# Head norm of an attention unit placed in the next unit's softmax, key rounded before the next weight piece, rotation product order exchanged

## The chip, the cores and the metric

The kernel runs on one core of one Trainium2 chip. The metric is the time of one execution in microseconds (us). Three executions of the kernel before took 3260.85, 3261.77 and 3262.95 us, so its median is 3261.77 us.

The engines named below are TensorE (PE, matrix products into PSUM), VectorE (DVE), ScalarE (ACT), GpSimd (POOL) and SyncE (SP, which issues the loads of the weights). SBUF is the working memory, PSUM the memory that TensorE writes. Each engine works through its own list of instructions in order; between engines, semaphores say what is ready.

## The reference

Two transformer blocks are applied one after the other to 512 tokens of width 1024, each with two layers. The change touches only the first block's differential attention (four heads, each with two score maps):

```python
def differential_attention(q, k, v, lam_full, subln_g, lambda_init):
    ...
        s = jnp.einsum('bqhcd,bkhcd->bhcqk', qblk, kk, preferred_element_type=jnp.float32) * scale
        p = jax.nn.softmax(s, axis=-1)
        a = p[:, :, 0] - lam_full * p[:, :, 1]
        return jnp.einsum('bhqk,bkhe->bqhe', a.astype(v.dtype), v)
    o = lax.map(block, qb)
    ...
    o = rms_norm(o, subln_g, SUBLN_EPS) * (1.0 - lambda_init)
    return o.reshape(B, S, H * 2 * Dh)
```

Queries and keys get a rotary embedding first:

```python
def apply_rope(t, cos, sin):
    ...
    t1, t2 = tf[..., :half], tf[..., half:]
    return jnp.concatenate([t1 * c - t2 * s, t2 * c + t1 * s], axis=-1).astype(t.dtype)
```

The dilated attention that follows uses the same embedding. Everything is float32.

## The kernel before, in words

**Layout.** Activations stand transposed: features on the 128 partitions, the 512 tokens along the free dimension. Every large product is computed by `gemm` (L451) as three products of split numbers: each operand is a rounded part ("Hi") and what is left ("Lo"), and TensorE computes Hi*Hi, Lo*Hi and Hi*Lo, so a projection of 128 output features is 8 x 3 = 24 matmuls of 128x512, written to one of the two slots of the PSUM tile `psG`.

**Weight pieces.** A projection reads one weight piece ("chunk") of 128x1024. SP loads pieces into a ring of four (`wring`), ACT rounds a piece (`cut_high`, L418, called by `follow`, L420, which first waits until the projection of an earlier piece is done), POOL subtracts (`cut_rest`, L440, tile `wLo`). Two cut pieces are held at a time. `follow(act, c, ...)` cuts piece c+2. SP reloads a slot of the ring when POOL has cut its piece.

**A unit.** The first block's layer has four units of differential attention, one per head (`attend(i)`, a loop on every engine; both layers run them). A unit's order on TensorE is: scores 0 and 1 (eight matmuls), gate projection, transposes of the value, scores 2, transposes 0 of the softmax, scores 3, query projection of the next head ("Q"), transposes 1 and 2, half of the key projection of the next head ("K"), transposes 3, second half of K, the attention output (`d_OUT`, L856), half of the value projection ("V"), two small sums of squares for the head norm (L864), second half of V. The scores and the transposes are numbered 0 to 3 by their block of 128 queries. Transposes 3 are the boundary that the prediction counts from; their row is the second of the two with L827 that have a wait after the query projection.

**The softmax of a unit.** DVE: `largest(n)` (L1341, largest score, from PSUM). ACT: `expo(n)` (L1055). DVE: `combine(n)` (L1349 to L1354: one over the sums, times lambda, the two maps scaled and added; tile `soft`). Then TensorE transposes (L827) and ACT copies out (`out_T`, L1062). `combine(n)` lets transposes n go.

**Rotary embedding.** ACT copies a projection from PSUM in four pieces of 32 partitions, exchanged (`rope_turn`, L1011, tile `tmp`). DVE's `rope_add` (L1301) multiplies that copy by the sine table (L1303), the projection in PSUM by the cosine table (L1304, tile `ra`), and adds (L1311, tile `qk`). The multiplication that reads PSUM frees its `psG` slot. TensorE's V projection needs the slot that K leaves.

**The next unit's scores** need the split query and key: ACT rounds (`cut_q`, L1026; `cut_k`, L1034, tile `kHi`), DVE subtracts (`rest_q`, L1318; `rest_k`, L1325, tile `kLo`).

**The head norm of a unit.** ACT squares the attention output (L1093) and copies it to `oaT`; TensorE sums over the head's 128 features (L864); ACT takes the root (L1101, two halves); DVE takes the reciprocal of each half (L1379, 128x256) and multiplies `oaT` (L1381). `oaT` of all four heads is read only after the dilated attention.

Nothing but the written order of each engine's code and the semaphores sets the order of the work.

## Time and profile before

| | |
|---|---|
| median of three executions | 3261.77 us |
| the profiled execution's own time | 3261.97 us |
| its span, first to last instruction | 3260.1 us |
| outside of the span | 1.9 us |
| mean granted clock of TensorE | 0.996 of full speed |
| TensorE busy | 3181.9 us, 98% |
| VectorE busy | 1641.8 us, 50% |
| ScalarE busy | 1343.6 us, 41% |
| GpSimd busy | 1373.1 us, 42% |

The busy times are sums over the whole span. They say which engine has the most work in total, not which one a stage waits for: that stands in the rows with an idle time and the name of what ended it. The differential attention takes from about 46 to 190 us in the first layer, and from about 1021 to 1165 us in the second.

### The profile page before, as it was taken

The page shows a single profiled execution, that of the slowest core. Times are in us where ns is not written, and L with a number is a line of the kernel's source. Part 1 is how long each engine was busy: PE and PEld are TensorE (multiplying, and loading weights), DVE is VectorE, ACT ScalarE, POOL GpSimd, SP SyncE. Part 2 cuts the span into 40 slices and gives each one's busy share as a digit, 9 for nine tenths or more (in the row PEclk, how much of TensorE's full clock was granted, in tenths as well). Part 3 has the DMA queues.
Part 4 walks back from the last instruction along what each step waited for, and adds up shares of the span by engine and source line. Part 5 has one row for each costly group of instructions (what it writes and reads, how often), then busy time and mean ns, then how long its engine had stood idle before and what let it go on. Part 6 is the DMA issues. An engine that isn't in the chain of part 4 may idle for free. (4 is left out here: it accounts for less than half of the span.)

```text
span 3260.1 us, 45286 instructions
## 1 busy us (share of the span) xinstructions
PE 3181.9 (98%) x15946; PEld 2534.8 (78%) x15946; DVE 1641.8 (50%) x2597; ACT 1343.6 (41%) x2108; POOL 1373.1 (42%) x694
## 2 busy tenths in 40 slices
PE   9999999999999999999999999999999999999999
PEld 6778887788887778887788886777888867778887
DVE  6853337655627853337656624863333248533332
ACT  6765554322226765554322224453222244532222
POOL 3233334544453223334444454544444535444444
PEclk9999999999999999999999999999999999999999
DMA  3122222255522122222255523202223232122222
GB/s 141 58 81 88 81 87 78 104 184 202 188 102 80 58 81 88 87 82 76 103 197 189 193 97 107 78 27 78 97 97 101 99 112 72 33 84 97 95 98 90
DMA packets 93593, 333.26 MB, mean 102 GB/s; under 512 B 10864, under 2 KB 12080, under 8 KB 93232
## 3 DMA queue, kind: packets, MB, share of 16 engines
q1 hardware_dynamic: 91760, 325.52, 28.9%
q10 hardware_dynamic: 1728, 6.36, 0.5%
q8 instruction: 64, 1.05, 0.1%
q14 instruction: 41, 0.34, 0.0%
HBM read 329.69 MB, written 8.44 MB: 104 GB/s over the span
## 5 line engine op out<-in xcount | busy, mean ns | idle before, releaser
L440 POOL TENSOR_TENSOR wLo<-wring,wHi 128x1024 fp32r<-128x1024 f32 x482 | 1174.2, 2436 | 1709.4 <-ACT wHi L418 1709.1
L464 PE MATMUL psG<-hHi,wHi 128*128 128x512 f32 x2992 | 1184.6, 396 | 12.6 <-DVE ra L1304 4.3
L464 PE MATMUL psG<-hLo,wHi 128*128 128x512 f32 x2992 | 1170.1, 391 | 9.1 <-POOL hLo L489 8.2
L464 PE MATMUL psG<-hHi,wLo 128*128 128x512 f32 x2992 | 1165.9, 390 | 0.0
L418 ACT ACTIVATE wHi<-wring 128x1024 fp32r<-128x1024 f32 x482 | 510.2, 1059 | 964.3 <-PE psG L464 934.6
L464 PEld LDWEIGHTS psG<-hHi,wHi 128*128 128x128 f32 x2992 | 562.3, 188 | 152.9 <-issue 33.2
L464 PEld LDWEIGHTS psG<-hLo,wHi 128*128 128x128 f32 x2992 | 561.7, 188 | 141.2 <-POOL hLo L489 23.4
L464 PEld LDWEIGHTS psG<-hHi,wLo 128*128 128x128 f32 x2992 | 562.7, 188 | 113.1 <-issue 0.5
L464 PE MATMUL psG<-hidLo,wHi 128*128 128x512 f32 x704 | 273.9, 389 | 0.0
L464 PE MATMUL psG<-hidHi,wHi 128*128 128x512 f32 x704 | 273.9, 389 | 0.0
L464 PE MATMUL psG<-hidHi,wLo 128*128 128x512 f32 x704 | 273.9, 389 | 0.0
L2340 DVE TENSOR_TENSOR tmp<-tmp,psG 128x512 f32<-128x512 f32 x44 | 30.3, 688 | 298.5 <-PE psG L464 298.5
L1303 DVE TENSOR_TENSOR tmp<-tmp,ropes 128x512 f32<-128x512 f32 x64 | 44.3, 692 | 253.0 <-ACT tmp L1011 253.0
L1011 ACT ACTIVATE tmp<-psG 32x512 f32<-32x512 f32 x256 | 151.1, 590 | 30.8 <-PE psG L464 27.4
L464 PEld LDWEIGHTS psG<-hidHi,wHi 128*128 128x128 f32 x704 | 132.1, 188 | 28.0
L464 PEld LDWEIGHTS psG<-hidHi,wLo 128*128 128x128 f32 x704 | 132.1, 188 | 27.3
L464 PEld LDWEIGHTS psG<-hidLo,wHi 128*128 128x128 f32 x704 | 132.1, 188 | 27.2
L1409 DVE CUSTOM_DVE_ANT_0 soft<-psS,mask 128x768 f32<-128x768 f32 x64 | 61.0, 953 | 154.6 <-issue 154.6
L1484 DVE CUSTOM_DVE_ANT_0 modw<-modw,cb 128x1024 f32<-128x1024 f32 x96 | 131.7, 1372 | 4.7
L1494 DVE TENSOR_TENSOR tmp<-tmp,psG 128x512 f32<-128x512 f32 x44 | 30.3, 688 | 183.7 <-PE psG L464 183.7
L2344 DVE TENSOR_TENSOR hidLo<-tmp,hidHi 128x512 f32 x44 | 118.3, 2689 | 5.4
L1498 DVE TENSOR_TENSOR hidLo<-tmp,hidHi 128x512 f32 x44 | 110.4, 2508 | 5.4
(321 smaller groups left out, 3374.3 us busy)
## 6 DMA issues: line engine op xcount, KB each, us to landing
wring<-in_w SPq DMA_DIRECT2D x490, 512.0 KB, 3.2
modw<-in_wmod SPq DMA_DIRECT2D x96, 512.0 KB, 5.5
e_copies<-e_rows ACTq DMA_DIRECT2D x8, 512.0 KB
T_tab<-e_copies SPq DMA_DIRECT2D x4, 1024.0 KB, 5.5
mask<-in_mask SPq DMA_DIRECT2D x2, 1536.0 KB, 6.0
xin_sb<-in_x SPq DMA_DIRECT2D x4, 512.0 KB, 5.1
e_copies<-e_rows ACTq DMA_DIRECT2D x8, 256.0 KB
out<-o_sb SPq DMA_DIRECT2D x4, 512.0 KB, 2.6
```

Source lines behind the costliest of these rows:

```text
L418: act.activation(wHi[:, c % CUTS, :, :], wring[:, c % RING, :, :], ACT.Copy).then_inc(w_high, 1)
L440: pool.tensor_tensor(wLo[:, c % CUTS, :, :], wring[:, c % RING, :, :], wHi[:, c % CUTS, :, :], ALU.subtract).then_inc(w_cut[c % CUTS], 1)
L464: mm = pe.matmul(psG[:, G.slot(u), :], w[:, c % CUTS, k, :], r(j), start=start and j == 0 and n == 0, stop=stop and j == len(kts) - 1 and ...
L1011: ins = act.activation(rot[32 * a:32 * a + 32, slot, :], ps[32 * b:32 * b + 32, :], ACT.Copy, scale=QSCALE[slot])
L1303: dve.tensor_tensor(rot[:, slot, :], rot[:, slot, :], ropes[:, :], ALU.mult)
L1409: dve.tensor_tensor_reduce(Sm[:, s, :], psS[:, S.slot(u), 0:DL_KEYS], mask[:, n // 2, :], 1.0, -3.0e38, ALU.add, ALU.max, stat[:, s, 0:1]) ...
L1484: dve.tensor_tensor_reduce(modw[:, j % 2, :], modw[:, j % 2, :], cb[:, :], 1.0, 0.0, ALU.mult, ALU.add, small[:, 9 + j % 4:10 + j % 4]).th ...
L1494: dve.tensor_tensor(sl[:, j, :], sl[:, j, :], psG[:, G.slot(u), :], ALU.mult).then_inc(G.emptied(u), 1)
L1498: dve.tensor_tensor(hidLo[:, k, :], sl[:, j, :], hidHi[:, k, :], ALU.subtract).then_inc(hid_full, 1)
L2340: dve.tensor_tensor(tmp[:, j, :], tmp[:, j, :], psG[:, G.slot(u), :], ALU.mult).then_inc(G.emptied(u), 1)
L2344: dve.tensor_tensor(hidLo[:, k, :], tmp[:, j, :], hidHi[:, k, :], ALU.subtract).then_inc(hid_full, 1)
```

## The change

Three things are written otherwise.

1. **Rotation.** `rope_add` issues the multiplication that reads PSUM first, and the one by the sine table second; the second now signals the engine's own counter, on which the addition waits. This holds for all 32 rotations of a layer.
2. **Key before weight piece.** On ACT the cut of the piece that follows K (`follow(CH1_DA + 6, ...)`) is no longer behind K's `rope_turn`. It stands behind `cut_k`. It is the piece of the next unit's gate projection.
3. **Head norm.** The two reciprocals and the multiplication of `oaT` of units 0 to 2 leave the end of the unit and go between the instructions of the next unit's softmax. `largest(2)` moves behind `combine(1)` in all units. The last unit of a layer keeps its own head norm at the end and does unit 2's as well. The PSUM slot of the sums is freed by ACT after the root. DVE's four units are now written as a first one, a loop of two and a last one; before, they were a loop of three and a last one.

```diff
                             rope_turn(j, psG[:, G.slot(u), :], i * 2 + j + 3)
-                            follow(act, CH1_DA + 5 + j, u, i, 4, GK_DA)
+                            if j == 0:
+                                follow(act, CH1_DA + 5, u, i, 4, GK_DA)
...
                         if not last:
                             cut_k(i * 2 + 4)
+                        follow(act, CH1_DA + 6, g_DA + d_K, i, 4, GK_DA)
                         act.preload_act_table(ACT.Sqrt)
                         for b in range(2):
...
                             act.activation(rms[:, 256 * b:256 * b + 256], psT[:, T.slot(u), 0:256], ACT.Sqrt,
                                            bias=eps[:, 1:2], scale=1.0 / P).then_inc(rms_full, 1)
+                            act.wait_ge(rms_full, i * 2 + b + 2)
+                            act.sem_inc(T.emptied(u), 1)
...
                     def rope_add(slot, ps, emptied, n_rots, o, classes):
                         until(dve, rot_full, n_rots)
-                        dve.tensor_tensor(rot[:, slot, :], rot[:, slot, :], ropes[:, :], ALU.mult)
-                        ins = dve.scalar_tensor_tensor(ra[:, :], ps, QSCALE[slot], ropec[:, :], ALU.mult, ALU.mult)
-                        ins.then_inc(emptied[0], 1)
+                        dve.scalar_tensor_tensor(ra[:, :], ps, QSCALE[slot], ropec[:, :], ALU.mult, ALU.mult).then_inc(emptied[0], 1)
+                        did(dve.tensor_tensor(rot[:, slot, :], rot[:, slot, :], ropes[:, :], ALU.mult))
                         until(dve, *emptied)
...
-                    def attend(i, last):
+                    def attend(i, first, last):
...
+                        def subnorm_inverse(i, b):
+                            half = slice(256 * b, 256 * b + 256)
+                            until(dve, rms_full, i * 2 + b + 2)
+                            did(dve.reciprocal(rstd[:, half], rms[:, half]))
+
+                        def subnorm_scale(i):
+                            dve.scalar_tensor_tensor(oaT[:, i, :], oaT[:, i, :], sub_g, rstd[:, :], ALU.mult, ALU.mult).then_inc(o_full, 1)
+
                         largest(0)
                         largest(1)
                         combine(0)
+                        if not first:
+                            subnorm_inverse(i - 1, 0)
+                        combine(1)
                         largest(2)
-                        combine(1)
+                        if not first:
+                            subnorm_inverse(i - 1, 1)
                         largest(3)
                         combine(2)
+                        if not first:
+                            subnorm_scale(i - 1)
                         combine(3)
                         next_rope(0, d_Q)
                         next_rope(1, d_K)
...
-                        for b in range(2):
-                            u, half = t_DA + 4 + b, slice(256 * b, 256 * b + 256)
-                            until(dve, rms_full, i * 2 + b + 2)
-                            dve.reciprocal(rstd[:, half], rms[:, half]).then_inc(T.emptied(u), 1)
-                            until(dve, *T.is_read(u, i, TK_DA))
-                        dve.scalar_tensor_tensor(oaT[:, i, :], oaT[:, i, :], sub_g, rstd[:, :], ALU.mult, ALU.mult).then_inc(o_full, 1)
                         if last:
+                            subnorm_inverse(i, 0)
+                            subnorm_inverse(i, 1)
+                            subnorm_scale(i)
...
-                    with dve.Fori(0, DA_HEADS - 1) as i:
-                        did.enter(i, 16)
-                        attend(i, False)
-                        did.leave(DA_HEADS - 1)
-                    attend(DA_HEADS - 1, True)
+                    attend(0, True, False)
+                    with dve.Fori(0, DA_HEADS - 2) as n:
+                        did.enter(n, 20)
+                        attend(n + 1, False, False)
+                        did.leave(DA_HEADS - 2)
+                    attend(DA_HEADS - 1, False, True)
```

How the instructions stand in a row. On VectorE, at the first two rotations of a layer (`tmp` is ACT's exchanged copy, `ra` the product that reads PSUM, `qk` the sum), before:

```order
L1303 TENSOR_TENSOR tmp<-tmp,ropes 128x512
L1304 SCALAR_TENSOR_TENSOR ra<-psG,ropec 128x512
L1311 TENSOR_TENSOR qk<-ra,tmp 128x512
L1303 TENSOR_TENSOR tmp<-tmp,ropes 128x512
L1304 SCALAR_TENSOR_TENSOR ra<-psG,ropec 128x512
L1311 TENSOR_TENSOR qk<-ra,tmp 128x512
```

and now:

```order
L1307 SCALAR_TENSOR_TENSOR ra<-psG,ropec 128x512
L1308 TENSOR_TENSOR tmp<-tmp,ropes 128x512
L1314 TENSOR_TENSOR qk<-ra,tmp 128x512
L1307 SCALAR_TENSOR_TENSOR ra<-psG,ropec 128x512
L1308 TENSOR_TENSOR tmp<-tmp,ropes 128x512
L1314 TENSOR_TENSOR qk<-ra,tmp 128x512
```

The two products have changed places; the lines are four lower in the file.

On ScalarE, in the loop over the units, behind the query's and key's projections (`wHi` is the rounded weight piece, `qBoth` and `kHi` the rounded query and key, `sq` and `oaT` the attention output); a minus stands for before, a plus for now:

```order
 L1011 ACTIVATE tmp<-psG 32x512 x4
-L237 REGISTER_ALU
-L418 ACTIVATE wHi<-wring 128x1024
 L1026 ACTIVATE qBoth<-qk 64x512 x2
...
 L1034 ACTIVATE kHi<-qk 64x512 x4
-L1097 ACT_TABLE_LOAD
-L1101 ACTIVATE rms<-psT,eps 128x256 x2
+L237 REGISTER_ALU
+L418 ACTIVATE wHi<-wring 128x1024
+L1099 ACT_TABLE_LOAD
```

The rounding of the weight piece has moved behind the rounding of the key and stands ahead of the table load for the root.

On VectorE, from the start of the last unit of a layer, whose softmax stands as in the middle ones (`stat` holds largest scores and sums, `soft` the softmax, `rstd` the reciprocals of the head norm), before:

```order
L1341 TENSOR_REDUCE stat<-psS 128x2 x2
L1349 RECIPROCAL stat<-stat 128x2
L1350 TENSOR_SCALAR stat<-stat,small 128x1
L1353 TENSOR_SCALAR soft<-soft,stat 128x512
L1354 SCALAR_TENSOR_TENSOR soft<-soft,stat 128x512
L1341 TENSOR_REDUCE stat<-psS 128x2
L1349 RECIPROCAL stat<-stat 128x2
L1350 TENSOR_SCALAR stat<-stat,small 128x1
L1353 TENSOR_SCALAR soft<-soft,stat 128x512
L1354 SCALAR_TENSOR_TENSOR soft<-soft,stat 128x512
L1341 TENSOR_REDUCE stat<-psS 128x2
```

and now:

```order
L1344 TENSOR_REDUCE stat<-psS 128x2 x2
L1352 RECIPROCAL stat<-stat 128x2
L1353 TENSOR_SCALAR stat<-stat,small 128x1
L1356 TENSOR_SCALAR soft<-soft,stat 128x512
L1357 SCALAR_TENSOR_TENSOR soft<-soft,stat 128x512
L1369 RECIPROCAL rstd<-rms 128x256
L1352 RECIPROCAL stat<-stat 128x2
L1353 TENSOR_SCALAR stat<-stat,small 128x1
L1356 TENSOR_SCALAR soft<-soft,stat 128x512
L1357 SCALAR_TENSOR_TENSOR soft<-soft,stat 128x512
L1344 TENSOR_REDUCE stat<-psS 128x2
L1369 RECIPROCAL rstd<-rms 128x256
```

One reciprocal of 128x256 stands ahead of `combine(1)`, one behind `largest(2)`, and `largest(2)` is behind `combine(1)`.

## Rows read from the trace of the kernel before

**Rows 1.** The page: busy time of each engine, share of the span, instructions.

```profile
PE 3181.9 (98%) x15946; PEld 2534.8 (78%) x15946; DVE 1641.8 (50%) x2597; ACT 1343.6 (41%) x2108; POOL 1373.1 (42%) x694
```

**Rows 2.** What TensorE waited for: us in total, times, longest.

```profile
PE psT L827 <- DVE soft L1354: 4.9, 10, 0.7
PE psG L464 <- DVE ra L1304: 4.3, 8, 0.5
PE psG L464 <- POOL wLo L440: 3.8, 6, 0.7
PE psS L818 <- DVE kLo L1325: 3.6, 6, 0.6
```

**Rows 3.** TensorE's timeline, units 0 and 1: start, duration, instruction, [idle before, releaser].

```profile
46.51 0.39 PE L818 MATMUL psS<-kHi,qBoth 128*128 128x512 f32 x1
...
81.26 0.49 PE L818 MATMUL psS<-kHi,qBoth 128*128 128x512 f32 x1 [0.61 <-DVE kLo L1325]
...
98.53 0.66 PE L827 MATMUL psT<-ident,soft 128*128 128x128 f32 x4 [0.20 <-DVE soft L1354]
...
102.27 0.63 PE L827 MATMUL psT<-ident,soft 128*128 128x128 f32 x4 [0.33 <-ACT PT L1062]
...
109.62 0.47 PE L464 MATMUL psG<-hHi,wHi 128*128 128x512 f32 x1 [0.54 <-DVE ra L1304]
...
116.84 0.49 PE L818 MATMUL psS<-kHi,qBoth 128*128 128x512 f32 x1 [0.61 <-DVE kLo L1325]
```

**Rows 4.** VectorE's timeline, end of unit 1.

```profile
108.18 0.69 DVE L1303 TENSOR_TENSOR tmp<-tmp,ropes 128x512 f32<-128x512 f32 x1 [3.67 <-ACT tmp L1011]
108.79 0.68 DVE L1304 SCALAR_TENSOR_TENSOR ra<-psG,ropec 128x512 f32<-128x512 f32 x1
109.50 2.74 DVE L1311 TENSOR_TENSOR qk<-ra,tmp 128x512 f32<-128x512 f32 x1
112.49 1.39 DVE L1318 TENSOR_TENSOR qBoth<-qk,qBoth 64x512 fp32r<-64x512 f32 x2 [0.24 <-DVE qk L1311]
113.91 2.79 DVE L1325 TENSOR_TENSOR kLo<-qk,kHi 64x512 fp32r<-64x512 f32 x4
```

**Rows 5.** ScalarE's timeline, end of unit 1.

```profile
108.17 1.06 ACT L418 ACTIVATE wHi<-wring 128x1024 fp32r<-128x1024 f32 x1
109.13 1.25 ACT L1026 ACTIVATE qBoth<-qk 64x512 fp32r<-64x512 f32 x2
...
110.91 0.59 ACT L1094 ACTIVATE oaT<-psG 128x512 f32 x1
112.28 2.57 ACT L1034 ACTIVATE kHi<-qk 64x512 fp32r<-64x512 f32 x4 [0.78 <-DVE qk L1311]
```

**Rows 6.** GpSimd's timeline: one piece of unit 0, two of unit 1, one after the units.

```profile
55.88 2.40 POOL L440 TENSOR_TENSOR wLo<-wring,wHi 128x1024 fp32r<-128x1024 f32 x1 [5.15 <-ACT wHi L418]
...
91.72 2.40 POOL L440 TENSOR_TENSOR wLo<-wring,wHi 128x1024 fp32r<-128x1024 f32 x1 [6.11 <-ACT wHi L418]
...
109.30 2.40 POOL L440 TENSOR_TENSOR wLo<-wring,wHi 128x1024 fp32r<-128x1024 f32 x1 [5.34 <-ACT wHi L418]
...
193.98 2.55 POOL L440 TENSOR_TENSOR wLo<-wring,wHi 128x1024 fp32r<-128x1024 f32 x1 [0.69 <-ACT wHi L418]
```

**Rows 7.** The norm's reciprocal: duration ns least/median/most, first and last start.

```profile
L1379 DVE RECIPROCAL rstd<-rms x16: 1752/1753/1755, 81.2 to 1161.3; 128x256 f32<-128x256 f32 x16
```

**Rows 8.** VectorE's timeline, unit 1: largest(2), the first scaling of combine(1).

```profile
90.66 1.22 DVE L1341 TENSOR_REDUCE stat<-psS 128x2 f32<-128x1024 f32 x1
...
92.66 1.74 DVE L1353 TENSOR_SCALAR soft<-soft,stat 128x512 f32<-128x512 f32 x1
```

**Rows 9.** ScalarE's timeline, unit 1: table load, expo(0), expo(3).

```profile
83.16 1.28 ACT L1071 ACT_TABLE_LOAD   x1
87.38 0.69 ACT L1055 ACTIVATE soft<-psS,stat 128x512 f32<-128x512 f32 x1 [2.94 <-DVEq L1343]
...
96.41 0.69 ACT L1055 ACTIVATE soft<-psS,stat 128x512 f32<-128x512 f32 x1 [2.46 <-DVEq L1343]
```

More of the change, by code:

```diff
@@ L1426, in _ @@
                     with dve.Fori(0, DL_PAIRS - 1) as n:
-                        did.enter(n, 8)
+                        did.enter(n, 14)
                         local(n + 1, False)
```

## The prediction

> **What bounds the kernel now.** I read the page first: TensorE is busy for 98% of the span, no other engine for more than 50% [rows 1]. So an edit on VectorE, ScalarE or GpSimd can only shorten the time where TensorE stands idle for it, and the next view is the list of what TensorE waited for. Four of its entries touch this change [rows 2]: transposes that wait for the softmax 4.9 us, the V projection waiting for `ra` 4.3, the scores waiting for `kLo` 3.6, weight pieces 3.8. The first three, 12.8 us, are all that the change aims at. Then come the timelines of unit 1, which sits between two like it: scores 0 at 81.26, transposes 2 at 98.53, transposes 3 at 102.27, V at 109.62, the next scores at 116.84 [rows 3]. Each has an idle time and a releaser. A unit takes 116.84 - 81.26 = 35.58 us, and I cut it at transposes 3: 21.01 us from scores 0 to there, 14.57 us from there to the next scores.
>
> A removed stall gives more than its idle time. The stalled matmul lasts 0.49 us, an unstalled one 0.39 [rows 3], and unstalled ones overlap (512 columns at the 2.4 GHz level are 0.21 us, so some 0.16 of the 0.39 lies beside the next; an estimate). I add 0.06 to 0.26 us per stall.
>
> **The rotation.** ACT's copy releases VectorE at 108.18. Now the product by the sine table goes first, 0.61 us, then `ra` ends at 109.47, and V starts 0.15 later [rows 3, 4]. Changed, `ra` ends at 108.86 and frees the slot for 109.01; TensorE was idle from 109.08. The stall goes: 0.54 + 0.06 = 0.6 us, 8 times. The extra wait of the addition on the engine's own counter costs a few hundredths on VectorE, which sits idle there for 3.67 us [rows 4]; nothing. The price is elsewhere: the sine product, with two SBUF inputs, now runs 0.61 us later and meets GpSimd. GpSimd's piece at 109.30 holds the addition that began at 109.50 until 112.24, that is 0.54 after the piece's end, where the same form takes 0.69 alone [rows 4, 6]. The other way round, a piece at 193.98 took 2.55 instead of 2.40 [rows 6]: GpSimd can be held too. TensorE waits for a weight piece twice a layer near a rotation (before K of unit 0 and after unit 3); there the piece begins about 0.2 us before the moved product ends. I charge +0.25 and +0.2 us per layer; the bounds are 0 and 0.69, the whole product.
>
> **The key ahead of the piece.** Behind K's copy ACT goes straight to `cut_q`, 0.96 us earlier (109.13 - 108.17), so the copy to `oaT` ends at 110.91 + 0.59 - 0.96 = 110.54 [rows 5]. GpSimd has no piece at 109.30 any more, so the addition runs free: 109.50 + 0.69 = 110.19 instead of 112.24. `cut_k` starts at 110.54 instead of 112.28 and ends at 113.11. On VectorE: 0.25 gap, `rest_q` to 111.84, first pair of `kLo` to 113.27, second pair to 114.67 (four in 2.79) [rows 4], instead of 116.70. With V 0.6 us earlier, TensorE is ready for scores at 116.84 - 0.6 - 0.61 - 0.26 = 115.37; `kLo` is there 0.6 us before. This stall goes too: 0.87 us. Together the stretch from transposes 3 to the scores shrinks by 1.47 us, to 13.10.
>
> The piece itself: its rounding ends at 113.11 + 1.06 = 114.17, GpSimd starts 0.07 later (109.23, 109.30). `kLo`'s last instruction begins at 113.97, a margin of 0.27 us, and holds GpSimd to 114.67; the piece is ready at 117.07. The gate projection wants it some 1.8 us after the scores began (eight matmuls), at 117.2. Just in time; cost 0 to 0.3 us. SP's reload of that ring slot starts 5 us later than before, with the use four pieces away: nothing.
>
> **The head norm.** Two reciprocals of 1.75 us [rows 7] and the product with `oaT` leave the place before `largest(0)`. Two things follow, times from the scores' start S:
> - ACT is then the later one. Before, `cut_k` ended at 114.85 and the exponential's table was there at 84.44 + 35.58 = 120.02, 5.17 us on [rows 5, 9]. Now it is 113.11 + 1.06 (piece) + 5.17 + 0.1 (new wait on the root) = 119.44 = S + 4.07. Before, expo(0) began at 87.38 = S + 6.12. combine(0) ended 3.28 us behind it (90.66 - 87.38) [rows 8, 9]: now S + 7.35. So the wait of transposes 0 (0.7 us, the larger share of the 4.9) goes.
> - Then the first reciprocal, to S + 9.1, and some 0.45 us of small instructions (from the end of `largest(2)` at 91.88 to the large scaling at 92.66 it is 0.78 with a wait in it [rows 8]): combine(1)'s large scaling wants to start at S + 9.55. But GpSimd takes the next piece in that moment. In unit 0, where nothing delays ACT, it began at 55.88, 9.37 us behind the scores at 46.51 [rows 3, 6]. So it begins at S + 9.37 and ends at S + 11.77, and the scaling is held, as in the row of 1.74 us that ends 0.28 behind the piece at 94.12 [rows 6, 8].
>
> Before, transposes 2 came 98.53 - 94.12 = 4.41 us behind the piece's end. Now two more things lie in that chain: `largest(2)`, 1.22 + 0.14, which stood ahead of combine(1), and the second reciprocal, 1.75 + 0.05. Sum 7.57. Transposes 2 come at S + 11.77 + 7.57 = S + 19.34 against S + 17.27 before. TensorE gets there at about S + 16 (17.27 less the stalls of 0.7 and 0.2 and their restarts) and stands idle for over 3 us. expo(3) started 2.12 us ahead of transposes 2 and 5.86 ahead of transposes 3 [rows 3, 9], of which 0.1 was slack: transposes 3 come at S + 19.34 - 2.12 + 5.76 = S + 22.98 against S + 21.01, +1.97 us. What VectorE gained at the start of the unit it pays back before its middle, behind the port and in front of TensorE. The 0.75 us product with `oaT` lies behind combine(2), where only combine(3) waits, due 1.5 us later: nothing. Unit 0 has no head norm to take over and no stall for the softmax: 0. In unit 3 its own norm stays at the end, behind a projection of the dilated stage: 0.
>
> The Trainium skill, "SBUF — State Buffer", section "Who interferes with whom", says that a VectorE instruction with two SBUF inputs, or in a two-port mode, and a GpSimd instruction that reads SBUF exclude each other, the first to start holding the ports. The rows of 1.74, 2.74 and 2.55 us agree. By the same rule the reciprocal, with one input, is free of it; its sixteen durations from 1752 to 1755 ns [rows 7], some of them beside a piece, agree. No row shows `kLo` or the sine product held, and the rule makes both liable: that is rivals C and D below.
>
> **Sum per layer:** +0.25 (first piece), 3 x -1.47, 3 x +1.97, -0.6 (last V), +0.2 (last piece) = +1.35. Two layers +2.7 us on the profiled execution's own 3261.97 us (span 3260.1 and 1.9 outside) gives 3264.7; the median is 0.2 below that execution, so **3264.5 us**.
>
> **The rivals.**
> - **B, combine(1) slips in before the piece.** It needs to be some 0.75 us earlier against GpSimd (its two large instructions, 0.5 and 0.75 us, both begun before S + 9.37). For it: my margin between the scaling and the piece is only 0.18 us, and ACT's table time is a sum of many terms. Against it: both terms would have to err in the same direction. Then transposes 0 and 2 do not wait, and the Q projection and what hangs on it come 0.71 + 0.16 earlier: -0.88 instead of +1.97. Per layer 0.25 - 4.41 - 2.64 - 0.6 + 0.2 = -7.2; time 3261.8 - 14.4 = 3247.4 us. This is also nearly all that the change can give.
> - **C, `kLo` loses the ports.** If the piece starts before `kLo`'s last instruction (margin 0.27 us), `kLo` ends at 114.24 + 2.40 + 0.54 = 117.18 and the scores start at 117.35, +0.51 instead of -1.47. But ACT and combine(1) are then nearly 2 us earlier against the scores, combine(1) is over by S + 9.2, and the unit runs as in B: 3 x (0.51 - 0.88). Per layer -1.5; time 3258.8 us, no change.
> - **D, both lose.** As C, but the piece comes between combine(1)'s two large instructions (by the numbers of C the second is over only 0.2 us before). The second is held to S + 11.77 + 0.54, and transposes 3 come +1.4. Per layer 0.25 + 3 x (0.51 + 1.4) - 0.6 + 0.2 = 5.6; time 3273 us, slower. It decides from an error of 0.3 us at the first place and 0.2 at the second.
> - **E, the PSUM slot is not what V waits for.** If another release ends 0.5 us later there, eight times 0.6 are missing: 3269.3 us. Against it: the row names `ra`, and 0.15 us from its end to V is what `kLo` shows as well (116.70, 116.84).
>
> **How the numbers follow.** Forecast (A) 0.56, B 0.17, C 0.12, D 0.10, E 0.05. I count as no change what is within 0.2%, about 6.5 us, since a measurement of this kernel can tell no less. A by itself reaches from 3259 to 3270: each 0.4 us of error in the chain behind the piece counts six times, 2.4 us. Of A 0.04 lie above the bound and 0.02 below; C is no change; E is half above. Faster 0.19, same 0.64, slower 0.17. A range with 8 in 10 must take in B and may leave out D: 3246 to 3270.
>
> **What would show it.** V without a stall, and `ra` gone from TensorE's waits. `qk` of K at 0.69 us and `kLo` ending about 0.6 us before the scores. A reciprocal between two scalings of `soft`, then combine(1)'s scaling at 2 us or more, ending 0.3 us behind a piece. TensorE's wait for `soft` at one place per unit, about 3 us, in units 1 to 3 and none in unit 0; the list's entry for L827 at some 18 us instead of 4.9. A unit of about 36 us. The forecast is wrong if that wait is under 1 us (B), or if the scores wait for `kLo` for over 1 us (C, D).

## The result, and the profile after

The changed kernel takes 3269.9 us in the median (3268.30 to 3278.14, eight runs), the kernel before 3261.91 us in the same series (3260.85 to 3264.10, eight runs). The ratio is 1.0025, with a 95% interval of 1.0015 to 1.0035: slower by 8 us. The forecast was 3264.5 us and no change; the measured time lies inside its range, just beyond the 0.2% that had been called no change.

The page of the kernel after has its span at 3267.8 us (the profiled execution took 3269.67 us) and this row of busy times, which answers to [rows 1]:

```profile
PE 3186.0 (97%) x15946; PEld 2543.4 (78%) x15946; DVE 1620.6 (50%) x2597; ACT 1346.3 (41%) x2108; POOL 1376.9 (42%) x694
```

TensorE is busy for 4.1 us more with the same 15946 instructions, so they do not all last as long as before, and it stands idle for the other 3.6 us by which the span has grown. What it waited for, in the kernel after, as in [rows 2]:

```profile
PE psT L827 <- DVE soft L1357: 18.5, 6, 3.2
...
PE psG L464 <- POOL wLo L440: 4.2, 6, 0.8
```

The entries for `ra` and `kLo` are gone; the wait for `soft` is 18.5 us in six places. TensorE's timeline of the kernel after, answering to [rows 3], with one row inside the stretch behind the stall:

```profile
79.95 0.39 PE L818 MATMUL psS<-kHi,qBoth 128*128 128x512 f32 x1
...
99.21 1.11 PE L827 MATMUL psT<-ident,soft 128*128 128x128 f32 x4 [3.22 <-DVE soft L1357]
...
100.97 0.63 PE L464 MATMUL psG<-hLo,wHi 128*128 128x512 f32 x1
...
103.80 0.60 PE L827 MATMUL psT<-ident,soft 128*128 128x128 f32 x4
...
110.55 0.47 PE L464 MATMUL psG<-hHi,wHi 128*128 128x512 f32 x1
...
116.98 0.39 PE L818 MATMUL psS<-kHi,qBoth 128*128 128x512 f32 x1
...
136.24 1.11 PE L827 MATMUL psT<-ident,soft 128*128 128x128 f32 x4 [3.22 <-DVE soft L1357]
...
173.16 0.66 PE L827 MATMUL psT<-ident,soft 128*128 128x128 f32 x4 [2.85 <-DVE soft L1357]
...
197.47 0.50 PE L464 MATMUL psG<-hHi,wHi 128*128 128x512 f32 x1 [0.69 <-POOL wLo L440]
```

V (110.55) and the scores (79.95, 116.98) start with no idle time. Transposes 2 come 19.26 us behind the scores, after 3.22 us of idling. Then the four transposes last 1.11 us, and a matmul of 128x512 lasts 0.63 us where it lasted 0.39. The windows of the kernel after say why. Each row is a stretch, its length, busy time and instructions of PE, PEld, DVE, ACT, POOL, and then the granted clock, DMA share and GB/s: ahead of unit 1's stall, the 3 us behind it, a stretch from there past the start of transposes 3, 3 us in unit 3 (from 0.3 us behind its stall on), and the whole differential attention of layer 1.

```profile
79.00:99.00 20.00, 16.99 (x81) 13.86 (x79) 14.39 (x19) 13.47 (x27) 7.11 (x3) 0.99 0.23 79
99.21:102.21 3.00, 3.00 (x9) 2.56 (x10) 2.80 (x7) 2.93 (x5) 0.11 (x1) 0.51 0.00 0
102.21:105.00 2.79, 2.79 (x16) 2.33 (x15) 2.67 (x2) 1.48 (x3) 2.79 (x1) 1.00 0.00 0
173.46:176.46 3.00, 3.00 (x11) 2.36 (x10) 2.89 (x7) 2.93 (x5) 0.23 (x1) 0.56 0.00 0
46.00:193.00 147.00, 136.94 (x588) 106.09 (x587) 101.76 (x134) 104.53 (x185) 42.52 (x17) 0.97 0.18 61
```

Behind each of the three long waits of the layer TensorE runs 3 us and more at half of full speed (0.51 to 0.56 in the windows), its lower level of 1.2 GHz instead of 2.4; so it does behind the three of the second layer. From transposes 2 to 3 of unit 1 it takes 4.59 us (4.59 = 103.80 - 99.21), where [rows 3] have 3.74 us with a wait of 0.33 in it. In units 2 and 3 it takes 4.85 and 4.84. The Trainium skill, "TensorE: Matmul & The Clock Gate", section "What's actually happening", says that a gate lets TensorE have either all or half of its clock pulses, and half when it has been idle. The windows of 0.51 and 1.00 agree with the two levels, and the 0.51 stands behind 3.22 us of idling; e7_nokey below has the same wait without the fall.

VectorE's timeline of the kernel after holds the rows that answer to [rows 4, 7, 8]:

```profile
73.97 0.69 DVE L1314 TENSOR_TENSOR qk<-ra,tmp 128x512 f32<-128x512 f32 x1
...
76.27 2.79 DVE L1328 TENSOR_TENSOR kLo<-qk,kHi 64x512 fp32r<-64x512 f32 x4
...
87.51 1.75 DVE L1369 RECIPROCAL rstd<-rms 128x256 f32<-128x256 f32 x1
...
89.94 1.89 DVE L1356 TENSOR_SCALAR soft<-soft,stat 128x512 f32<-128x512 f32 x1
91.87 0.75 DVE L1357 SCALAR_TENSOR_TENSOR soft<-soft,stat 128x512 f32<-128x512 f32 x1
92.53 1.22 DVE L1344 TENSOR_REDUCE stat<-psS 128x2 f32<-128x1024 f32 x1
93.97 1.75 DVE L1369 RECIPROCAL rstd<-rms 128x256 f32<-128x256 f32 x1 [0.22 <-DVE stat L1344]
95.76 1.22 DVE L1344 TENSOR_REDUCE stat<-psS 128x2 f32<-128x1024 f32 x1
```

and GpSimd's, answering to [rows 6]:

```profile
78.69 2.62 POOL L440 TENSOR_TENSOR wLo<-wring,wHi 128x1024 fp32r<-128x1024 f32 x1 [10.27 <-ACT wHi L418]
...
89.14 2.40 POOL L440 TENSOR_TENSOR wLo<-wring,wHi 128x1024 fp32r<-128x1024 f32 x1 [3.71 <-ACT wHi L418]
```

`kLo` ends at 79.06, 0.89 us ahead of the scores. The piece of 89.14 starts 9.19 us behind them; the scaling that wanted to run at 89.94 ends at 91.83, 0.29 behind the piece's end of 91.54. Behind it stand `largest(2)` and the second reciprocal, and only then the chain to transposes 2.

### The profile page after: what moved, and what is told of

Same layout as the page of the kernel before. It is cut to its first block and busy times, and to the rows that moved or that the text cites. A ratio compares the mean times of both kernels' runs of the same rounds, so it can differ in the third digit from the quotient of the medians.

```text
span 3267.8 us, 45350 instructions
## 1 busy us (share of the span) xinstructions
PE 3186.0 (97%) x15946; PEld 2543.4 (78%) x15946; DVE 1620.6 (50%) x2597; ACT 1346.3 (41%) x2108; POOL 1376.9 (42%) x694
## 5 line engine op out<-in xcount | busy, mean ns | idle before, releaser
L1307 DVE SCALAR_TENSOR_TENSOR ra<-psG,ropec 128x512 f32<-128x512 f32 x64 | 44.2, 691 | 253.2 <-ACT tmp L1011 253.2
```

The source lines that it names most:

```text
L1307: dve.scalar_tensor_tensor(ra[:, :], ps, QSCALE[slot], ropec[:, :], ALU.mult, ALU.mult).then_inc(emptied[0], 1)
```

## The experiments

T is in each expectation the theory of the forecast with what the result added to it: each edit is worth its wait at TensorE, the chain behind the held scaling sets transposes 2, and behind a long wait the granted clock may fall. Each kernel ran against the kernel before in the same job; the medians of that one were 3262.69, 3263.10 and 3262.76 us in the three jobs. All intervals are of 95%.

### Each part alone

**e1_rot**: the kernel before with the two products of the rotation exchanged, and no more.

```diff
-                        dve.tensor_tensor(rot[:, slot, :], rot[:, slot, :], ropes[:, :], ALU.mult)
-                        ins = dve.scalar_tensor_tensor(ra[:, :], ps, ...)
-                        ins.then_inc(emptied[0], 1)
+                        dve.scalar_tensor_tensor(ra[:, :], ps, ...).then_inc(emptied[0], 1)
+                        did(dve.tensor_tensor(rot[:, slot, :], rot[:, slot, :], ropes[:, :], ALU.mult))
```

> The kernel before with the rotation's two products exchanged and nothing else. Theory T (what decides is the chain behind each stall): V starts 0.6 us earlier, but the next scores wait for kLo, whose chain is not touched, so the 0.6 us are given back 6 of 8 times. -1.2 us for the last V of each layer, +0.9 for the moved product: 3261.6 us, and TensorE's wait for kLo grows from 0.6 to 1.2 us per unit. Rival R (each stall is worth its own time): 8 x -0.6 + 0.9 = 3258.0 us, wait for kLo unchanged.

Measured: 3261.84 us, ratio 0.9999 (0.9990 to 1.0008). The `ra` wait goes and comes back at the scores; TensorE's waits and one row of its timeline, in e1_rot:

```profile
PE psS L818 <- DVE kLo L1324: 7.5, 6, 1.3
```

```profile
117.74 0.49 PE L818 MATMUL psS<-kHi,qBoth 128*128 128x512 f32 x1 [1.25 <-DVE kLo L1324]
```

In [rows 2] it was 3.6 us. The exchange alone is worth nothing: `kLo` is next.

**e2_rotkey**: e1_rot and the key ahead of the weight piece.

```diff
-                            follow(act, CH1_DA + 5 + j, u, i, 4, GK_DA)
+                            if j == 0:
+                                follow(act, CH1_DA + 5, u, i, 4, GK_DA)
...
                             cut_k(i * 2 + 4)
+                        follow(act, CH1_DA + 6, g_DA + d_K, i, 4, GK_DA)
```

> Rotation exchanged and the key rounded ahead of the weight piece; the head norm stays where it was. Theory T: the stretch from transposes 3 to the scores shrinks by 1.47 us, but the roots are ready only as late as before, the two reciprocals and the product with oaT then stand alone in front of largest(0), which starts at S + 5.8 instead of S + 4.8; the wait for the softmax at transposes 0 grows from 0.7 to 1.7 us. Net about -0.5 per unit: 3259 us. Rival R: 8 x -0.6 and 6 x -0.87 with 0.9 back: 3252.8 us.

Measured: 3258.70 us, ratio 0.9991 (0.9982 to 1.0000): 4 us won, at the edge of what can be told. The waits for `ra` and `kLo` are gone, and a unit takes 34.98 us. But the head norm still stands ahead of `largest(0)` and now waits for ACT's roots, so TensorE waits longer at transposes 0, and at scores 2, where it had no wait. From VectorE's timeline, then TensorE's, in e2_rotkey:

```profile
80.44 3.54 DVE L1380 RECIPROCAL rstd<-rms 128x256 f32<-128x256 f32 x2 [1.37 <-ACT rms L1103]
```

```profile
88.25 0.50 PE L818 MATMUL psS<-kHi,qBoth 128*128 128x512 f32 x1 [0.53 <-ACT soft L1055]
...
90.24 0.65 PE L827 MATMUL psT<-ident,soft 128*128 128x128 f32 x4 [0.80 <-DVE soft L1355]
```

The size came as expected, the place partly: a wait of 1.7 us at transposes 0 had been expected, and it is two, of 0.53 and 0.80.

**e8_norot**: the change with the two products in their old order (the lines of e1_rot the other way round).

> The change with the rotation's part undone: V waits 0.54 us for ra again. Theory T: scores come 0.6 us later against ScalarE than in the change; combine(1)'s large scaling wants to start at S + 8.95, runs before the piece, and its second instruction at S + 9.47 is held by the piece: transposes 2 at S + 18.9, idle 2.8 us, clock down as in the change: 3273 us. If combine(1) slips through as a whole (it needs 0.1 us): 3251 us. Rival (the rotation's part is a gain by itself): 3269.9 + 4.8 - 0.9 = 3274 us with an idle time of 3.2 us unchanged.

Measured: 3272.62 us, ratio 1.0031 (1.0018 to 1.0043), 2.7 above the whole change, which the two intervals do not tell apart. The number is close to T's 3273, the way is not T's: combine(1)'s large scaling was to run before the piece, at S + 8.95, and in unit 1 it came at S + 9.39, 0.20 us behind the piece's start, and was held. The wait there is 3.21 us, as the rival had it (3.2). The `ra` waits are back, 4.5 us in 8. In one unit `kLo` lost the ports, which is the mechanism of rival C. VectorE's, GpSimd's and TensorE's timelines in e8_norot:

```profile
114.55 5.01 DVE L1329 TENSOR_TENSOR kLo<-qk,kHi 64x512 fp32r<-64x512 f32 x4
```

```profile
116.62 2.39 POOL L440 TENSOR_TENSOR wLo<-wring,wHi 128x1024 fp32r<-128x1024 f32 x1 [10.35 <-ACT wHi L418]
```

```profile
119.69 0.49 PE L818 MATMUL psS<-kHi,qBoth 128*128 128x512 f32 x1 [1.15 <-DVE kLo L1329]
...
135.26 1.19 PE L827 MATMUL psT<-ident,soft 128*128 128x128 f32 x8
```

Four instructions that take 2.79 us alone take 5.01 with a piece across them, the scores come late, and for that the unit has no stall at transposes 2, all three as C had it.

**e7_nokey**: the change with the piece's cut behind K's `rope_turn` again (the lines of e2_rotkey the other way round).

> The change with the key's part undone: the weight piece is cut ahead of the key again. Theory T: scores wait for kLo 1.2 us (the kernel before: 0.6) and start where they did in the kernel before, but ScalarE's exponentials are then 0.7 us earlier against them, combine(1)'s large scaling wants to start at S + 8.8 and its second instruction at S + 9.3, just before GpSimd's piece at S + 9.37; both run free, transposes 2 come at S + 16.5 nearly without a wait and at full clock: 3257 us, faster than the change although a stall comes back. Rival (the key's part is a gain by itself): its 6 x 0.87 are lost, 3275 us.

Measured: 3278.66 us, ratio 1.0048 (1.0033 to 1.0062). T missed by 22 us, on a race at the port that it had called the wrong way: the scaling came at S + 9.41 where T had S + 8.8. The rival, the key's part as a gain by itself, had 3275. VectorE's and GpSimd's timelines in e7_nokey:

```profile
91.04 2.58 DVE L1354 TENSOR_SCALAR soft<-soft,stat 128x512 f32<-128x512 f32 x1
```

```profile
90.94 2.40 POOL L440 TENSOR_TENSOR wLo<-wring,wHi 128x1024 fp32r<-128x1024 f32 x1 [4.39 <-ACT wHi L418]
```

The scaling came 0.10 us after the piece and was held; that the chain would have been free had it come first is T's argument and not shown. T's S + 8.8 is the S + 9.55 of the prediction less 0.7. In the change the scaling had been seen at S + 9.99, and from there the 0.7 lead to S + 9.3, beside the piece (S + 9.37 expected): nothing to forecast a winner from. TensorE's timeline in e7_nokey has the wait for `kLo` and the stall too:

```profile
81.63 0.49 PE L818 MATMUL psS<-kHi,qBoth 128*128 128x512 f32 x1 [1.16 <-DVE kLo L1326]
...
101.00 0.66 PE L827 MATMUL psT<-ident,soft 128*128 128x128 f32 x4 [3.22 <-DVE soft L1355]
```

Behind the same 3.22 us of idling the transposes last 0.66 us here, not 1.11: the clock did not fall, as its window shows, and transposes 3 follow after 3.58 us (104.58) instead of 4.59. So it was in all three places of this layer; in the second layer, in the same execution, the clock fell behind the first two waits (3.21 and 3.22 us) and not behind the third.

```profile
101.00:104.00 3.00, 3.00 (x15) 2.56 (x16) 2.80 (x7) 2.93 (x5) 0.11 (x1) 1.00 0.00 0
```

### The chain in front of transposes 2

**e3_l2**: the change with `largest(2)` ahead of `combine(1)` again.

```diff
-                        combine(1)
                         largest(2)
+                        combine(1)
                         if not first:
                             subnorm_inverse(i - 1, 1)
```

> The change with one thing undone: largest(2) ahead of combine(1) again. Theory T: largest(2) then lies beside the weight piece that holds combine(1), so only the second reciprocal is left in the chain behind the piece: 4.41 + 1.80 = 6.2 us, transposes 2 at S + 18.0 instead of S + 19.3, wait 1.9 us instead of 3.2, that is 6 x -1.36 = -8.2 us. If the idle time is what lowers TensorE's clock and 1.9 us is too short for it, another 6 x -1.1: 3255 us. If the clock falls all the same: 3262 us. Rival R (the order of largest(2) does not matter, the held scaling does): 3270 us.

Measured: 3257.21 us, ratio 0.9981 (0.9972 to 0.9990). One `largest` out of the chain cuts the stall of unit 1 by 1.42 us (1.36 in the prediction's sum) and brings 12.7 us over six units: 2.1 us each, the clock included, which now mostly stays up. That lies between T's two numbers, 3255 with the clock up and 3262 with it down. TensorE's timeline in e3_l2:

```profile
99.16 0.66 PE L827 MATMUL psT<-ident,soft 128*128 128x128 f32 x4 [1.80 <-DVE soft L1357]
...
133.88 0.87 PE L827 MATMUL psT<-ident,soft 128*128 128x128 f32 x4 [1.91 <-DVE soft L1357]
```

and the windows behind the second of the two:

```profile
133.90:134.90 1.00, 1.00 (x5) 0.98 (x6) 0.88 (x3) 0.99 (x2) 0.00 (x0) 0.64 0.00 0
134.90:135.90 1.00, 1.00 (x4) 0.73 (x3) 0.93 (x2) 0.96 (x3) 0.00 (x0) 0.50 0.00 0
```

Of the three stalls in layer 1 (1.80, 1.91, 1.57 us) one brought the clock down, of the three in layer 2 (1.79, 1.89, 1.56 us) none.

**e6_inv1late**: the change with `largest(2)` left behind `combine(1)`, the second reciprocal behind `combine(2)` and the product behind `combine(3)`.

```diff
                         largest(2)
-                        if not first:
-                            subnorm_inverse(i - 1, 1)
                         largest(3)
                         combine(2)
                         if not first:
-                            subnorm_scale(i - 1)
+                            subnorm_inverse(i - 1, 1)
                         combine(3)
+                        if not first:
+                            subnorm_scale(i - 1)
```

> The change with only the second reciprocal moved behind combine(2) and the product with oaT behind combine(3); largest(2) stays behind combine(1). Theory T: the chain behind the piece is 4.41 + 1.36 = 5.8 us, transposes 2 at S + 17.5, an idle time of 1.4 us and no fallen clock: 6 x -1.8 and -7 for the clock: 3252 us. Rival (each of the two things moved into the chain costs only its overlap, the reciprocal nothing): 3262 us or more.

Measured: 3256.67 us, ratio 0.9979 (0.9970 to 0.9988). Taking only 1.8 us out of the chain wins 13.2 us, so the chain set the time. The stall of unit 1 is 1.88 us shorter, six times that is 11.3 us, and the clock fell behind none of the six waits (1.10 to 1.34 us). T had 4.7 us less: it gave transposes 3 no wait, and they wait for ACT's copies. TensorE's timeline in e6_inv1late:

```profile
97.66 0.66 PE L827 MATMUL psT<-ident,soft 128*128 128x128 f32 x4 [1.34 <-DVE soft L1357]
...
101.71 0.63 PE L827 MATMUL psT<-ident,soft 128*128 128x128 f32 x4 [0.65 <-ACT PT L1062]
```

**e4_late**: both, that is `largest(2)`, `combine(1)`, `largest(3)`, `combine(2)`, second reciprocal, `combine(3)`, product.

```diff
-                        combine(1)
                         largest(2)
-                        if not first:
-                            subnorm_inverse(i - 1, 1)
+                        combine(1)
                         largest(3)
                         combine(2)
                         if not first:
-                            subnorm_scale(i - 1)
+                            subnorm_inverse(i - 1, 1)
                         combine(3)
+                        if not first:
+                            subnorm_scale(i - 1)
```

> As before this one, and the second reciprocal behind combine(2), the product with oaT behind combine(3). Theory T: the chain behind the piece is as it was in the kernel before (4.4 us), transposes 2 would come at S + 16.2, where TensorE arrives at about S + 16: no wait over 0.3 us, full clock, a unit of about 33.3 us: 3248 us. Rival: combine(3) or the copies on ScalarE are then late for transposes 3, which wait over 1 us: 3254 us or more.

Measured: 3247.03 us, ratio 0.9960 (0.9946 to 0.9974). VectorE's timeline in e4_late:

```profile
89.18 1.22 DVE L1344 TENSOR_REDUCE stat<-psS 128x2 f32<-128x1024 f32 x1
...
91.18 0.49 DVE L1356 TENSOR_SCALAR soft<-soft,stat 128x512 f32<-128x512 f32 x1
```

`largest(2)` now lies beside the piece (88.95 to 91.35) and still lasts 1.22 us, and the scaling, which by the records starts 0.17 us before the piece's end, is not held. This is nearly the time that the prediction gave to rival B (3247.4 us), reached by another way: there combine(1) was to be early, here it is late and harmless.

**e11_cutlater**: the change with the gate's piece cut behind `expo(2)`, so that it cannot meet combine(1).

```diff
-                        follow(act, CH1_DA + 4, u, i, 4, GK_DA)
                         u = g_DA + d_VT
...
                         expo(2)
+                        follow(act, CH1_DA + 4, g_DA + d_GATE, i, 4, GK_DA)
                         out_T(0)
```

> The change with the gate's weight piece cut on ScalarE behind expo(2) instead of ahead of the value's copy. Theory T (GpSimd's piece holds combine(1)'s large scaling): combine(1) runs free and ends at S + 10.9, largest(2), the reciprocal and largest(3) follow to S + 15.4, and now combine(2)'s large scaling is held by the later piece (S + 14.8 to 17.2): transposes 2 at S + 18.3 instead of 19.3, 6 x -1.1 us, and some of the fallen clock with it: 3258 to 3263 us. Rival (the scaling of 1.9 us is long for another reason): it stays long, 3270 us.

Measured: 3264.07 us, ratio 1.0004 (0.9995 to 1.0013). VectorE's timeline in e11_cutlater:

```profile
89.87 0.49 DVE L1356 TENSOR_SCALAR soft<-soft,stat 128x512 f32<-128x512 f32 x1
...
96.41 1.08 DVE L1356 TENSOR_SCALAR soft<-soft,stat 128x512 f32<-128x512 f32 x1
```

combine(1)'s scaling is free, 0.49 us. The piece, later now, holds combine(2)'s scaling instead, and the stall is 2.44 us in place of 3.22. Freed of 1.40 us at the one place and held for 0.59 us at the other, the chain is 0.8 us shorter: all that moving this piece is worth in the chain. `largest(2)` and the second reciprocal still stand in it. The time lies 1 us above the expected 3258 to 3263. Behind the six waits of 2.41 to 2.49 us the clock fell four times, in units 1 and 3 of each layer, and stayed up in units 2.

### The clock behind the stall

**e5_awake**: the change with twelve matmuls of 128x512, whose results nobody reads, between transposes 1 and 2. They only keep TensorE busy.

```diff
                         turn(1)
+                        pe.wait_ge(w_cut[(CH1_DA + 6) % CUTS], ...)
+                        pe.wait_ge(*G.is_free(g_DA + d_K, i, GK_DA))
+                        for _ in range(AWAKE):
+                            pe.matmul(psG[:, G.slot(g_DA + d_K), :], wHi[:, (CH1_DA + 6) % CUTS, 0, :], hHi[:, 0, :], start=True, stop=True)
                         turn(2)
```

> The change, with twelve matmuls of 128x512 added on TensorE in each unit between transposes 1 and transposes 2, where it stood idle for 3.2 us; their result is overwritten and nothing waits for them. They take 12 x 0.23 = 2.8 us. Theory T (the idle time is what lowers the clock, and the lowered clock costs 1.2 to 1.4 us behind each of the six stalls): transposes 2 come no earlier, the granted clock stays at its upper level, 3269.9 - 7 = 3263 us. Rival (the clock falls for another reason, or the slow matmuls behind the stall are a restart cost and not the clock): 3270 us or more.

Measured: 3268.23 us, ratio 1.0020 (1.0010 to 1.0029), against 3263 expected. What was left out in that sum is unit 0, where TensorE has no idle time there: the twelve matmuls make its scores-to-scores time 35.27 us instead of 33.44, in the second layer too, 3.7 us in all. The remaining 1.5 us stay open. In units 1 to 3 they did what was expected, TensorE's timeline in e5_awake:

```profile
97.91 3.02 PE L850 MATMUL psG<-hHi,wHi 128*128 128x512 f32 x12
...
101.38 0.66 PE L828 MATMUL psT<-ident,soft 128*128 128x128 f32 x4 [0.46 <-DVE soft L1362]
...
137.44 0.66 PE L828 MATMUL psT<-ident,soft 128*128 128x128 f32 x4 [0.43 <-DVE soft L1362]
```

A unit takes 137.44 - 101.38 = 36.06 us, with transposes 2 as late behind the softmax as in the kernel after, where it takes 136.24 - 99.21 = 37.03 us. The fallen clock of unit 1 costs 0.97 us. From transposes 2 of unit 2 to those of unit 3 it is 35.70 us instead of 36.92, so there it costs 1.22.

**e10_awake3**: the same, with the twelve matmuls only in units 1 to 3.

```diff
+                        if awake:
+                            pe.wait_ge(...)
...
-                    with pe.Fori(0, DA_HEADS) as i:
-                        attend(i)
+                    attend(0, 0)
+                    with pe.Fori(0, DA_HEADS - 1) as n:
+                        attend(n + 1)
```

> As e5_awake, with the twelve matmuls only in units 1 to 3, where TensorE stands idle; in unit 0, which has no such idle time, they cost 2.2 us a layer. Theory T: a unit takes 36.06 us as in e5_awake instead of 37.03, transposes 2 come no earlier: 3269.9 - 6 x 1.0 = 3263.5 us, granted clock at its upper level behind transposes 2. Rival (the gain of e5_awake in a unit is something else than the clock): 3268 us or more.

Measured: 3265.14 us, ratio 1.0006 (0.9997 to 1.0015). Transposes 2 come at 102.24 and 138.28, a unit takes 36.04 us again (36.06 expected), and behind the short wait the clock is up, the window in e10_awake3:

```profile
99.90:102.90 3.00, 2.54 (x14) 1.86 (x13) 2.45 (x7) 2.75 (x7) 0.00 (x0) 1.00 0.00 0
```

With the clock held up the change costs about what the prediction's sum says (3264.5 us); without, 3269.9. The profiled execution, 3266.36 us, is one of the slower ones: ahead of the attention its clock was down for longer (0.66 from 10 to 30 us, 0.91 in the kernel after), and its first scores start at 49.64 us instead of 46.51.

### A faster order

**e9_best**: e4_late, and ACT's copy of transposes 1 ahead of the weight piece behind the query's rotation, for the waits that e4_late had left for ACT (4.6 us in 8).

```diff
                             if j == 0:
+                                out_T(1)
                                 follow(act, CH1_DA + 5, u, i, 4, GK_DA)
...
                         next_rope(0, d_Q)
-                        out_T(1)
                         out_T(2)
```

> The kernel e4_late with transposes' copy 1 (out_T(1)) on ScalarE ahead of the weight piece that follows the query's rotation. In e4_late transposes 3 wait 0.4 to 0.7 us for that copy in each of the eight units. Theory T: the copy ends 1.1 us earlier, the piece 0.6 later with its use a projection away; the wait goes, 8 x -0.6 with the restart: 3242 us. Rival (the piece is then late for V, or VectorE's rotation behind it): 3247 us or more.

Measured: 3243.79 us, ratio 0.9943 (0.9929 to 0.9956): the fastest of all, 19 us under the kernel before and 26 under the change. The wait for ACT at transposes 3 is gone; in units 1 and 2 one of 0.31 us for the softmax is in its place. TensorE's timeline in e9_best, and the window from 46 to 193 us, as above for the kernel after:

```profile
99.79 0.66 PE L827 MATMUL psT<-ident,soft 128*128 128x128 f32 x4 [0.31 <-DVE soft L1357]
```

```profile
46.00:193.00 147.00, 145.38 (x643) 112.61 (x642) 102.52 (x141) 113.44 (x197) 49.06 (x20) 1.00 0.22 73
```

In the same 147 us the kernel after had 136.94 us of TensorE's work at a clock of 0.97, this one 145.38 at 1.00. A unit takes 33.10 us.

## Why the prediction was right in its mechanism and wrong in its verdict

**Right.** The rotation frees V (no stall, `ra` gone), and alone it is worth nothing, since `kLo` follows (e1_rot). The key ahead of the piece frees the scores; `kLo` is 0.89 us early, forecast 0.6. ACT is the later one at the start of the unit: expo(0) came 4.32 us behind the scores, forecast 4.07. The piece starts at S + 9.19 (forecast 9.37), the scaling is held and ends 0.29 behind the piece (0.28). Transposes 2 come at S + 19.26 (19.34), the stall is "over 3 us" at 3.22, and the list's entry is 18.5 us ("some 18"). e3_l2 and e6_inv1late took the two added terms out one at a time, and each shortened the stall of unit 1 by its own size: 1.42 us (1.36) and 1.88 us (1.80).

**Rivals.** B did not come about: combine(1)'s large scaling came at S + 9.99 (forecast 9.55), 0.80 us behind the piece's start, where the margin had been put at 0.18. Of C, one unit of e8_norot shows the mechanism; in the change itself the piece meets `kLo` only for GpSimd to be held (2.62 us). D was seen nowhere. E is ruled out: V starts with no idle time once `ra` is early. C's sum has a slip: its terms give 0.25 - 1.11 - 0.6 + 0.2 = -1.3 per layer, not -1.5, so 3259.3 us and not 3258.8; nothing hangs on it.

**The step that failed.** It is the +1.97 us per unit behind the held scaling. The sum priced the stall at its idle time and let transposes 3 follow transposes 2 by 5.76 - 2.12 = 3.64 us, as at full speed; a fallen clock behind the stall it put at nothing, without a reason. Measured are 4.59, 4.85 and 4.84 us in units 1 to 3 of the first layer and 4.75, 4.85 and 4.82 in the second: the granted clock was 0.5 behind each stall. That is 0.95 to 1.21 us more in each of the six, 6.9 us in all. It is the clock and not the wait as such: in e7_nokey the same wait of 3.22 us with the clock up leaves 3.58 us to transposes 3, and the twelve matmuls of e5_awake and e10_awake3 give back 0.97 and 0.99 us of unit 1's 37.03.

By layers: +1.35 forecast, +4.13 and +4.27 measured. In the first layer the projection behind unit 3 starts at 193.34 before and 197.47 after. From the first scores to that projection the kernel before takes 146.8 us in both layers, the kernel after 150.96 and 151.09, e10_awake3 147.60 and 147.62. So the clock is 3.4 us of it per layer, and with the clock up the change costs 0.8 there, where the sum without its first term has 1.1. What the sum charged too much has two main parts. In unit 3 transposes 2 came at S + 18.91, 0.43 us earlier than forecast. For the moved product TensorE's wait ahead of K in unit 0 grew from 0.70 to 0.81 us and the one behind unit 3 from 0.59 to 0.69, 0.2 us per layer where 0.45 were charged, and the first scores of layer 1 still start at 46.51. Outside of these stretches the kernel after took 0.7 us less. This is why its profiled execution (3269.67 us) lies only 5.0 us above the sum.

The prediction had the means to see it. It put an idle time of over 3 us in front of TensorE where the kernel before had no wait for the softmax above 0.7 us [rows 2], and it gave that only its length. And the kernel before does have waits of that length elsewhere, four in the whole trace (2.88 to 3.13 us, at L569, in the norms). The clock fell at each: the 3 us behind their ends show 0.61, 0.50, 0.54 and 0.50. The third of the four, from TensorE's timeline and the windows of the kernel before:

```profile
1968.08 1.88 PE L569 MATMUL psT<-rstd,spread 128*128 128x128 f32 x8 [2.90 <-PEq L1626]
```

```profile
1968.08:1971.08 3.00, 3.00 (x15) 3.00 (x16) 1.40 (x4) 0.21 (x1) 0.81 (x6) 0.54 0.40 108
```

The kernel's own text has a helper `keep_awake` (L544), which issues extra matmuls of an identity tile right behind L569 (L793, L1628). A chance of the clock falling belonged among the rivals, on the slower side.

**The verdict.** With the clock held up the change measures 1.0006 (e10_awake3), no change as forecast. With the fall it is 1.0025. The fall is not a matter of the profiled execution alone: all eight executions of the kernel after have a mean granted clock of 0.992 to 0.994, those of the kernel before in the three jobs 0.994 to 0.998. That the median still lies inside the range, by 0.1 us, is luck: the range reached up to 3270 for errors in the chain, and a fallen clock was not among its reasons.

**Open.** What decides whether the clock falls behind a wait. By kernels, in the profiled executions: in the kernel after it fell in six of six places (2.85 to 3.22 us), in e7_nokey in two of six (2.85 to 3.22), in e8_norot in three of five (2.83 to 3.21), in e11_cutlater in four of six (2.41 to 2.49), in e3_l2 in one of six (1.56 to 1.91), in e6_inv1late in none of six (1.10 to 1.34). Below 2 us it fell once in twelve, above 2.4 us fifteen times in twenty-three. The length alone does not tell: in e11_cutlater it fell behind waits of 2.41 to 2.44 us and stayed up behind both of 2.49. The median of e7_nokey lies 3.9 us above its profiled execution (3274.74 us). The mean granted clock, 0.995 in that one and 0.993 or 0.994 in the other four, fits executions in which the clock falls more often; no trace shows where.

## What to carry to other kernels

Price a new wait of the engine that sets the end twice: by its length, and by what its clock does behind it, here 3 us and more at half speed and 1.0 to 1.2 us lost for each wait of about 3 us. Look first whether the trace already has a wait of that length, and what the clock did behind it. When work is moved off one place, write down the chain that it joins: between the last instruction that another engine holds and the one that the busiest engine waits for, each microsecond counts in full. Put such work behind the instruction that is waited for. The same edits, ordered so, made 8 us of loss into 16 us of gain (e4_late), and moving one copy on ScalarE made it 19 (e9_best).

## What the runs showed of the hardware

- TensorE's granted clock was 0.5 for 3 us and more behind waits of 2.85 to 3.22 us, and fell behind four of 2.41 to 2.44 us and one of 1.91 us; 128x512 matmuls then lasted 0.63 us instead of 0.39 and started every 0.43 instead of every 0.23. It does not happen each time.
- A product over only 64 partitions (`kLo`) is held by GpSimd's piece as well: 5.01 us for four instead of 2.79. So is the sine product of 128x512: 2.37 instead of 0.68 us once in e11_cutlater.
- GpSimd is held too: a piece of 2.40 us took 2.62 behind `kLo` and up to 2.90 at 102.10 us in the kernel after.
- A scaling of `soft` that meets a piece ends 0.29 us behind the piece's end, in the change and in e11_cutlater alike, while reciprocals of 128x256 stay at 1.74 to 1.75 us wherever they lie. In e7_nokey the two start within 0.1 us of each other, and the expectation, which had the scaling first, lies 22 us from the measurement.
